# Running sums of stick-breaking attention from a rounded operand and its remainder, in a two-layer decoder kernel

## The reference, cut to what matters

```
z = einsum('bqhd,bshd->bhqs', qb, k) * HEAD_DIM ** -0.5
log_beta = log_sigmoid(z)
log_1m = where(strict, log_sigmoid(-z), 0.0)
log_rem = cumsum(log_1m, axis=3, reverse=True) - log_1m
a = where(strict, exp(log_beta + log_rem), 0.0)
out = einsum('bhqs,bshd->bqhd', a, v)
```

## Time and profile before

| | |
|---|---|
| median of 3 runs | 618.19 us (618.13 to 618.28) |
| the profiled execution: its time | 618.07 us |
| its span | 616.3 us |
| TensorE busy | 603.6 us (98%) |
| VectorE busy | 412.9 us (67%) |
| ScalarE busy | 339.6 us (55%) |
| GpSimd busy | 25.9 us (4%) |

### The profile page before, as it was taken

How to read it: one execution, slowest core, us unless ns; L and a number is a source line. 1 busy time by engine, 2 the same in 40 slices (tenths; PEclk the granted TensorE clock), 3 DMA queues, 4 the chain that set the end, 5 groups by cost and what they waited for, 6 DMA issues and landing times.

```text
span 616.3 us, 10303 instructions
## 1 busy us (share of the span) xinstructions
PE 603.6 (98%) x3729; PEld 527.5 (86%) x3729; DVE 412.9 (67%) x668; ACT 339.6 (55%) x631; POOL 25.9 (4%) x49
## 2 busy tenths in 40 slices
PE   7999999999999999999999999999999999999995
PEld 6988887798888888888899999878988888888884
DVE  4698746677756655665886676667776556666546
ACT  5776767265654554455556666653655544555430
POOL 0102012020000000000020000002000000000000
PEclk9999999999999999999999999999999999999999
DMA  8876434446755565555438434451775665556401
GB/s 270 271 237 242 137 103 135 173 148 223 244 176 185 186 204 187 183 187 192 138 115 278 162 130 138 136 209 66 263 231 191 204 203 183 184 181 202 137 1 68
DMA packets 31203, 109.48 MB, mean 178 GB/s; under 512 B 3440, under 2 KB 4464, under 8 KB 31040
## 3 DMA queue, kind: packets, MB, share of 16 engines
q1 hardware_dynamic: 29600, 102.77, 50.2%
q0 software_dynamic: 1568, 6.23, 2.9%
HBM read 107.94 MB, written 1.05 MB: 177 GB/s over the span
## 4 chain that ended last, share of the span: by engine, by line
PE 91%; DMA 3%; DVE 2%; ACT 2%; SPq 1%; issue 1%; DVEq 0%; POOL 0%
PE bank L976 27%; PE bank L892 24%; PE bank L954 12%; PE bank L895 12%; DMA raw<-stream_in 3%; PE bank L906 3%; PE bank L933 2%; PE bank L885 2%; PE bank L1025 2%; PE bank L1036 1%; PE bank L1016 1%; DVE wlo L605 1%; PE bank L939 1%; PE bank L1223 1%; ACT whi L334 1%
## 5 line engine op out<-in xcount | busy, mean ns | idle before, releaser
L605 DVE TENSOR_TENSOR wlo<-raw,whi 128x1024 fp32r<-128x1024 f32 x190 | 226.5, 1221 | 68.1 <-ACT whi L334 67.9
L334 ACT CAST whi<-raw 128x1024 fp32r<-128x1024 f32 x190 | 192.5, 1049 | 22.7 <-DMA raw<-stream_in 22.4
L892 PE MATMUL bank<-hTs,whi 128*128 128x512 f32 x640 | 160.1, 392 | 0.0
L892 PEld LDWEIGHTS bank<-hTs,whi 128*128 128x128 f32 x640 | 116.1, 189 | 21.4
L976 PE MATMUL bank<-whi,oThi 128*128 128x512 f32 x240 | 94.9, 395 | 0.0
L976 PE MATMUL bank<-whi,oTlo 128*128 128x512 f32 x240 | 93.7, 390 | 0.0
L976 PE MATMUL bank<-wlo,oThi 128*128 128x512 f32 x240 | 93.5, 390 | 0.0
L895 PEld LDWEIGHTS bank<-hTs,wlo 128*128 128x128 f32 x640 | 87.3, 190 | 6.3
L895 PE MATMUL bank<-hTs,wlo 128*128 128x256 f32 x640 | 89.2, 282 | 0.0
L954 PE MATMUL bank<-hTs,whi 128*128 128x256 f32 x320 | 60.6, 289 | 0.0
L976 PEld LDWEIGHTS bank<-whi,oThi 128*128 128x128 f32 x240 | 45.1, 188 | 10.0 <-issue 1.5
(11 more groups left out here) (153 smaller groups left out, 701.5 us busy)
## 6 DMA issues: line engine op xcount, KB each, us to landing
raw<-stream_in SPq DMA_DIRECT2D x190, 512.0 KB, 4.5
qT<-ln_rows_in POOLq DMA_DIRECT2D x8, 512.0 KB, 5.1
v<-xT_in SPq DMA_DIRECT2D x4, 256.0 KB, 4.8
kT<-stream_in SPq DMA_DIRECT2D x4, 256.0 KB, 5.0
h<-x_in POOLq DMA_DIRECT2D x1, 1024.0 KB, 7.2
out<-h SPq DMA_DIRECT2D x4, 256.0 KB, 2.0
dist<-consts_in POOLq DMA_DIRECT2D x1, 384.0 KB, 3.6
ukv<-w_uk_in POOLq DMA_DIRECT2D x1, 256.0 KB, 5.6
```

The source lines that it names most:

```text
L334: nc.scalar.copy(whi[:, c % RING, j * HW:(j + 1) * HW], raw[:, c % RAW, j * HW:(j + 1) * HW]).then_inc(whi_ready, 1)
L605: nc.vector.tensor_tensor(wlo[:, c % RING, cols], raw[:, c % RAW, cols], whi[:, c % RING, cols].bitcast(F32), ALU.subtract).then_inc(wlo_r ...
L892: mm(dst[:], whi[:, slot, off + k * P:off + (k + 1) * P], hTs[:, k].rearrange("p j s -> p (j s)"), start=(k == 0), stop=False)
```

## The change

The masked sp is split like the weights. ScalarE casts it to fp32r (`sphi`), VectorE subtracts (`splo`). Each of the three products is done twice, on `sphi` and on `splo`, against a triangle and ones that have been copied to fp32r tiles once (their entries, 0 and -1, are exact there). All products are then fp32r. The cast and the subtraction of a pair stand in the slot after its scores: on ScalarE after the evacuations and ahead of the split of the chunk, on VectorE as the first thing of the slot. `sphi` lies in parts of `oThi` and `oTlo` that are free until A pair 2 and 3, `splo` in the first 384 columns of `zeros` and a new tile, the triangle in the last 128 columns of `zeros`.

```diff
+        sp_rest = sb("sp_rest", [P, TRI], F32R)
+        ones = sb("ones", [P, P], F32R)
+        sphi = [t[:, 2:4, :].rearrange("p k s -> p (k s)")[:, 0:TRI] for t in (oThi, oTlo)]
+        splo = [zeros[:, 0:TRI], sp_rest[:]]
-        negtri = dist[:, TRI:TRI + P]
-        negones = dist[:, TRI + P:TRI + 2 * P]
+        negtri, negones = zeros[:, TRI:TRI + P], ones[:]
...
             evac_proj(2, 2, qT[:, 0:2, :], DH ** -0.5)
+            nc.scalar.copy(negtri, dist[:, TRI:TRI + P])
+            nc.scalar.copy(negones, dist[:, TRI + P:TRI + 2 * P]).then_inc(tri_ready, 1)
             split_hi(5)
...
                     evac_probT(2 * T_AT[s])
+                if s - 1 in Z_AT:
+                    for n in (2 * Z_AT[s - 1], 2 * Z_AT[s - 1] + 1):
+                        act.wait_ge(sp_masked, n + 1)
+                        if n >= 2:
+                            act.wait_ge(rem_done, n - 1)
+                        nc.scalar.copy(sphi[n % 2], scratch[:, 2 + n % 2, :]).then_inc(sphi_ready, 1)
...
             for s in range(SLOTS0):
+                if s - 1 in Z_AT:
+                    for n in (2 * Z_AT[s - 1], 2 * Z_AT[s - 1] + 1):
+                        dve.wait_ge(sphi_ready, n + 1)
+                        nc.vector.tensor_tensor(splo[n % 2], scratch[:, 2 + n % 2, :],
+                                                sphi[n % 2].bitcast(F32), ALU.subtract).then_inc(splo_ready, 1)
...
             def stick_rest(m):
+                pe.wait_ge(tri_ready, 1)
                 for n in (2 * m, 2 * m + 1):
-                    sp_t, z = scratch[:, 2 + n % 2, :], bank[n % 2]
-                    pe.wait_ge(sp_masked, n + 1)
-                    mm(z[:, 0:S], negtri, sp_t[:, 0:S], start=False, stop=False, skip_group_check=True)
-                    mm(z[:, P:S], negones, sp_t[:, S:TRI], start=False, stop=False, skip_group_check=True)
-                    mm(z[:, S:TRI], negtri, sp_t[:, S:TRI], start=False, stop=True, skip_group_check=True
-                       ).then_inc(rem_done, 1)
+                    z = bank[n % 2]
+                    for part, sp_t in enumerate((sphi[n % 2], splo[n % 2])):
+                        pe.wait_ge(splo_ready if part else sphi_ready, n + 1)
+                        mm(z[:, 0:S], negtri, sp_t[:, 0:S], start=False, stop=False, skip_group_check=True)
+                        mm(z[:, P:S], negones, sp_t[:, S:TRI], start=False, stop=False, skip_group_check=True)
+                        last = mm(z[:, S:TRI], negtri, sp_t[:, S:TRI], start=False, stop=part == 1,
+                                  skip_group_check=True)
+                    last.then_inc(rem_done, 1)
```

More of the change, by code:

```diff
@@ L156, in build @@
             sem("rinv_ready"), sem("pnorm_ready"), sem("oThi_ready"), sem("oTlo_ready"))
+        sphi_ready, splo_ready, tri_ready = sem("sphi_ready"), sem("splo_ready"), sem("tri_ready")
         z_done, absz_ready, e_ready, l_ready, sp_ready, sp_masked, rem_done, a_exp, a_masked = (
```

## The result

The changed kernel takes 620.63 us (median of 7 executions, 619.06 to 622.85), against 618.19 us before (7 executions, 618.01 to 618.82). The medians lie 2.4 us apart; the ratio as recorded, which is not quite that of the medians, is 1.0042, with a 95% interval of 1.0025 to 1.006. A second series, of 12 executions of the changed kernel and 35 of the one before, gave 619.98 us against 618.41, 1.6 us apart, and a ratio of 1.0018 (1.0005 to 1.003). So the change costs about 1 to 3 us. The forecast was 618.2 us in a range of 617.2 to 621.3. The time is inside, but the likeliest case, no measurable change, was not what came; "slower" had 0.33.

The account below looks back on a forecast made before the run. TensorE, busy 603.6 of 616.3 us, was taken to bound the kernel. First-pair loss 0.7, other pairs' gain 1.2 and slot 14 loss 0.5 summed to 0.0 us: forecast 618.2 us, range 617.2 to 621.3.

Parts of the forecast that it names:

- the likeliest case: Whole kernel: no change of note, under 0.2% (1.24 us), at 618.2 us; chance 0.43.
- slower: Whole kernel: slower by over 0.2%, from rival 1 and the rest of rival 3; chance 0.33.
- Part 1: TensorE's products: a head falls by 0.20 to 0.68 us; busy time over eight heads falls by 1.6 us.
- Rival 1: TensorE: the narrow fp32r product is worked off like f32, 0.22 us, giving 621.0 us; chance 0.30.
- Part 2: Per head one ScalarE cast of 0.50 us and one VectorE subtraction of 0.55; together 4 and 4.4 us.
- Part 3: First pair of heads, slots 0 to 2: TensorE waits for cast and subtraction, loss 0.7 us.
- Part 4: Other three pairs: remainders ready well ahead, gain 1.2 us; the 0.7 us wait in slot 10 stays.
- Part 5: Pair 3, slot 12: VectorE 1.5 us late, so TensorE waits for A pair 2's oTlo in slot 14, loss 0.5 us.
- Part 6: Two 128-column constant copies on ScalarE near 30.8 us: cost 0, or 0.6 us without the cover.
- rival 3: Handovers of the new chain or late normalised rows make the delay grow: 619.2 us; chance 0.12.
- the low case of rival 2: No wait in slot 14 and a narrow product of 0.06 us: 616.2 us; chance 0.05.

Follow-up runs that it names:

- the second profile: Profiled execution of the changed kernel run again with nothing edited: 619.67 us; median of that series 619.98 us, ratio 1.0018 against the kernel before.
- the first profile: Profiled execution of the changed kernel's first series: 622.85 us, the slowest of that series.
- the two filled kernels: Changed kernel with unused 256-column products in pair 0's waits: 618.84 us; the same idea with two extra ScalarE copies lengthening the first wait: 620.33 us.
- the one with f32 products: Changed kernel keeping its casts, subtractions and waits, but with three f32 products per head from the unsplit operand: 622.13 us, ratio 1.006.
- the longer standstill: Changed kernel with two more 384-column ScalarE copies ahead of pair 0's first rounded part: 620.97 us, ratio 1.0046.

## Why the prediction was right or wrong

**Part 1, the products: right.** Forecast 0.68 us a head, measured 0.64, with the narrow fp32r product at 0.09 to 0.11 us where I took 0.11. From the scores of A pair 0 to those of A pair 3, with pairs 1 and 2 between, the second profile takes 94.01 - 60.82 = 33.19 us against 93.19 - 59.17 = 34.02: 0.83 saved, 0.80 forecast. Rival 1, the narrow product at f32's price, is refuted, and with it 0.30 of the 0.33 that I had for "slower". That the time fell near its 621.0 us is chance.

**Part 2, the new operations: right.** A cast took 0.51 us where I had 0.50, a subtraction 0.55 as forecast. The busy time rose by 4.0 us on ScalarE and 4.1 on VectorE; forecast were 4 and 4.4.

**Part 3, the waits of pair 0: right in size, and the step that failed.** Forecast were two waits of 1.2 and 0.8 us, measured 1.3 and 0.5 (and 1.21 and 0.46). ScalarE idled 2.24 us before its first new cast and 1.37 before that of pair 3, where I had 2.3 and 1.4. The loss against before is 60.82 - 39.90 - (59.17 - 39.03) = 0.78 us where I had 0.7. But the step priced a standstill at its own length. It left out what TensorE's clock does behind one: in some executions it is granted 0.50 for several us, 3.4 us in the first profile. Its average share can only be estimated, from the mean clocks: 0.9957 over the 19 executions of the changed kernel against 0.9969 over the 83 of the kernel before, whose clock falls at times too, gives 0.0012 x 618 = 0.8 us; against 0.9974 over the 24 of the two filled kernels it would be 1.05. This term was missing in the sum.

The Trainium skill, "TensorE: Matmul & The Clock Gate", section "HAM oscillation — how this bites in real kernels", puts the fall of the clock down to idle gaps of TensorE, by its rule to gaps longer than any standstill in pair 0 here. In these runs the clock fell behind a single standstill of 2.11 us, and behind two of 1.3 and 0.5 us with three products between. That idle gaps bring the clock down agrees with the traces; where the page's rule and these runs differ, the runs decide.

**Part 4: right.** No wait appeared in slots 3 to 12, and the one in slot 10 stayed at 0.69 us.

**Part 5, what is late next: the mechanism was right, the place one slot early, the size 0.2 us small.** I followed the delay to the oTlo of A pair 2, asked for in slot 14, and overlooked that the values of A pair 2 in slot 13 wait for the oTlo before it, that of B pair 2. VectorE's timeline after, against the earlier trace rows:

```profile
101.59 0.55 DVE L631 SCALAR_TENSOR_TENSOR prob<-dsel,bank 128x384 f32<-128x384 f32 x1
...
105.20 0.42 DVE L657 TENSOR_TENSOR oTlo<-bank,oThi 128x256 fp32r<-128x256 f32 x1 [0.18 <-ACT oThi L375]
```

and TensorE's:

```profile
105.78 0.65 PE L1053 MATMUL bank<-probT,v 128*64 128x256 f32 x4 [0.73 <-DVE oTlo L657]
```

TensorE waits 0.73 us there and then comes late enough to slot 14 to find the next one ready. That the cause is the place of pair 3's casts and subtractions is shown from both sides: in f32 and in the later places the wait is gone. The wait that I had forecast in slot 14 exists behind the other: once slot 13 is free and the casts stay, in the later places, it is there with 0.19 us.

**Part 6, the constants: not tested by itself.** No wait that could be theirs appeared before slot 0. The start-up varied by more than they could cost.

**The sum.** Without a fall of the clock the stage grew by 0.33 us where I had 0.0. Behind the stage another 0.4 us were lost, which no step had: 617.9 - 104.95 = 512.95 us to the end of the span against 616.3 - 103.75 = 512.55. Nearly all of it is the normalisation. The list shows a wait of 0.2 us there, but the weight load of its first transposes waits 0.61 us where it waited 0.24 before. This wait appears in the eight profiles in which pair 0 has its casts and subtractions, also in the one with f32 products, and in none of the four without them; what links the two stays open. With the clock's estimated 0.8 us this makes 1.5 us. The two series gave medians 2.4 and 1.6 us apart, so the second is accounted for and about 1 us of the first is not. Without the clock's share the time would lie at 618.9 us, between the forecast and rival 3, the delay that grows on the way. How often the clock falls in pair 0 is known only roughly: the mean clocks don't say where it fell, and one of the low ones was a fall in the start-up.

That the range held the time is partly luck: its upper part rested on rival 1, which is refuted, and not on the clock. At the other end it left out the low case of rival 2, 616.2 us, to which I had given 0.05.

## What to carry to other kernels

A faster operation on the bounding engine is paid for by what feeds it: here 0.24 us a head came with a handover over two more engines, and where that had no filling in front it cost more than it gave. Split only the parts whose new steps lie in someone's idle time (pairs 1 to 3 here, with pair 3's steps moved: 618.51 to 617.41 us in one series), and look for every wait on a counter, also on the one before the item you follow, and on weight loads as well as on products. Price a new standstill of TensorE not only by its length: when it comes to the 1.8 to 2.4 us of these runs, compare the granted clock and the scatter over several executions, and put the kernel's own products into it.

## What the runs showed of the hardware

- TensorE's granted clock fell from 1.00 to 0.50 behind standstills of 2.11 us in one piece, of 1.78 us in the start-up, and of 1.3 and 0.5 us around three short products. It held behind one of 2.40 us and behind nearly the same pair, 1.21 and 0.46. The changed kernel went either way in two executions. A mean clock of 0.995 or less had 7 of 83 executions of the kernel before, 5 of 19 of the changed one, 4 of 10 with the longer standstill, 5 of 5 with the f32 products behind it, and 0 of 24 with the standstills filled.
- Products whose results nobody reads, laid into an existing wait, took 1.1 us off the median (619.98 to 618.84) with stages of 65.05 and 65.17 us in the two profiles.
- An fp32r product of 128 columns costs 0.09 to 0.11 us (two of them and one of 256 columns take 0.30 to 0.34), less than one of 256 columns (0.12), with a weight load for each. An f32 product of the same size takes 0.22.
